# Norm rates as a ScalarE root and a VectorE reciprocal, block by block; two up tiles side by side; the last two down pieces bank by bank

## What is computed

```python
def rmsnorm(t, w, eps):                     # also rms_norm
    return t * rsqrt(mean(t * t) + eps) * w
# first block
oa  = rmsnorm(diff_attention(qa, ka, va), subln_w)          # 8 heads of 128
qkv = silu(conv5(h @ w_in[qkv columns]))                    # 24 tiles of 128 channels
q, k = l2norm(q), l2norm(k)                                 # per head, 128 wide
... gated delta rule, mixer out, x += ..., x += mixture of experts ...
# second block
yn  = (y - mu) * rsqrt(var + eps); out = (yn + bonus) * g   # RWKV mixer
x   = x + rms_norm(merged @ w_out, post_mix_g)
hf  = rms_norm(x, pre_ffn_g)
u   = square(relu(hf @ w_up)) @ w_down
out = x + rms_norm(u, post_ffn_g)
```

## Time and profile before

| what | us |
|---|---|
| runs | 2788.33, 2776.55, 2788.61 |
| median | 2788.33 |
| profiled execution, its own time | 2778.82 |
| its span | 2777.0 |
| mean granted clock of TensorE | 0.973 |

### The profile page before, as it was taken

How to read it: one execution, slowest core, us unless ns; L and a number is a source line. 1 busy time by engine, 2 the same in 40 slices (tenths; PEclk the granted TensorE clock), 3 DMA queues, 4 the chain that set the end, 5 groups by cost and what they waited for, 6 DMA issues and landing times.

```text
span 2777.0 us, 34353 instructions
## 1 busy us (share of the span) xinstructions
PE 2557.9 (92%) x14425; PEld 1728.0 (62%) x14425; DVE 1034.7 (37%) x1699; ACT 799.8 (29%) x1308; POOL 678.5 (24%) x200
## 2 busy tenths in 40 slices
PE   8999989889999999898988889989998999999998
PEld 6856777687888543333323233337676878788887
DVE  4567866765232311011011110123468563260432
ACT  6567544524222010000100000032453232411212
POOL 3400644625543000000000000023132123344442
PEclk9999989989999999999999999999998999999999
DMA  5231112103236799999999999983120023332332
GB/s 167 91 54 70 53 62 91 61 4 120 91 107 242 291 406 428 427 427 428 429 427 427 429 428 427 426 322 121 62 72 5 17 84 121 107 99 91 98 99 76
DMA packets 131342, 554.53 MB, mean 200 GB/s; under 512 B 7240, under 2 KB 88592, under 8 KB 104720
## 3 DMA queue, kind: packets, MB, share of 16 engines
q1 hardware_dynamic: 131216, 552.72, 51.3%
HBM read 542.18 MB, written 10.52 MB: 199 GB/s over the span
## 4 chain that ended last, share of the span: by engine, by line
PE 69%; DMA 13%; DVE 8%; ACT 5%; issue 3%; POOL 2%; SPq 0%; DVEq 0%; ACTq 0%
DMA S<-in_w_up 11%; PE PS L2241 8%; PE PS L612 7%; PE PS L614 7%; PE PS L613 7%; PE PS L2208 7%; PE PS L2191 2%; PE PS L3586 2%; PE PS L3589 2%; PE PS L3588 2%; PE PS L2252 1%; PE PS L2708 1%; POOL r_block L487 1%; PE PS L621 1%; DMA S<-in_w_down 1%
## 5 line engine op out<-in xcount | busy, mean ns | idle before, releaser
L2208 PE MATMUL PS<-S 128*64 128x512 f32 x2032 | 453.3, 596 | 69.9 <-DMA S<-in_w_up 66.7
L612 PE MATMUL PS<-r_block,r_block 128*128 128x512 f32 x1024 | 405.9, 396 | 13.9 <-POOL r_block L487 5.1
L2583 POOL TENSOR_TENSOR r_block<-S,r_block 128x2048 fp32r<-128x2048 f32 (+1 forms) x63 | 277.9, 4412 | 511.0 <-ACT r_block L2573 465.7
L613 PE MATMUL PS<-r_block,r_block 128*128 128x512 f32 x1024 | 400.7, 391 | 0.0
L614 PE MATMUL PS<-r_block,r_block 128*128 128x512 f32 x992 | 388.5, 392 | 0.0
L2208 PEld LDWEIGHTS PS<-S 128*64 128x64 f32 x2032 | 140.0, 137 | 374.8 <-issue 247.1
L487 POOL TENSOR_TENSOR r_block<-S,r_block 128x2048 fp32r<-128x2048 f32 x48 | 222.5, 4636 | 448.8 <-ACT r_block L479 239.6
L2437 POOL TENSOR_TENSOR S<-S 128x1024 f32<-128x1024 f32 x4 | 9.5, 2387 | 978.2 <-DVE S L2425 978.2
L2241 PE MATMUL PS<-S 128*64 128x512 f32 x1024 | 229.0, 605 | 6.0 <-DMA S<-in_w_down 2.7
L612 PEld LDWEIGHTS PS<-r_block,r_block 128*128 128x128 f32 x1024 | 193.5, 189 | 59.8 <-issue 7.6
L613 PEld LDWEIGHTS PS<-r_block,r_block 128*128 128x128 f32 x1024 | 193.6, 189 | 40.0 <-issue 0.7
(11 more groups left out here) (521 smaller groups left out, 4045.0 us busy)
## 6 DMA issues: line engine op xcount, KB each, us to landing
S<-in_w_up SPq DMA_DIRECT2D x64, 2048.0 KB, 20.8
S<-in_w_down SPq DMA_DIRECT2D x64, 2048.0 KB, 25.7
S<-in_w_gate SPq DMA_DIRECT2D x63, 2048.0 KB, 18.0
S<-in_w_in SPq DMA_DIRECT2D x57, 1024.0 KB, 5.4
S<-in_w_up SPq DMA_DIRECT2D x16, 1024.0 KB, 5.4
S<-in_w_down SPq DMA_DIRECT2D x16, 1024.0 KB, 4.9
S<-decay_rows SPq DMA_DIRECT2D x8, 1024.0 KB, 7.0
S<-in_w_out SPq DMA_DIRECT2D x8, 1024.0 KB, 5.2
```

The costliest lines, as they stand in the source:

```text
L612: pe.matmul(out, wh, r32(HT[:, dc, :]), start=(dc == 0), stop=False)
L613: pe.matmul(out, wh, r32(low[:, dc, :]), start=False, stop=False)
L2208: mm = pe.matmul(PS[c * CAP:(c + 1) * CAP, 2 + 2 * m + g, :], XE[:, 2 * q + r, e * CAP:(e + 1) * CAP], w[:, r, 1024 * g + 512 * c:1024 * g ...
L2583: pool.tensor_tensor(r32(w), w, rounded(high2(name)), ALU.subtract).then_inc(sem("w2_low"), 1)
```

## The change

At five places the rate `1 / sqrt(v + eps)` was Ln and then Exp on ACT; now it is Sqrt on ACT and a reciprocal on DVE.

- End of attention: the reciprocal stands in front of the scaling on DVE.
- Groups: at `j` 11 the root stands ahead of the middle tap on ACT, a one-element Tanh behind it. On DVE the reciprocal, the scaling of the keys and `silu(10)` stand ahead of the four taps of tile 11. The first four copies of turned tiles stand ahead of `tanh(11)`.
- Second mixer: as at the end of attention.
- Post mix norm: per row block square, root, reciprocal and addition; the product with the weights goes to another buffer (`UW`), 3 fillers instead of 12, POOL waits for the last row block before it splits ("u", 0). Up tiles 0 and 1 run together: first all products with the high part of the weights (32), then the 16 with the low part. The pre-FFN norm has root and reciprocal of 128x4.
- End: the last two down pieces go bank by bank, both over banks 0 to 4 in turn, then both for each of 5, 6 and 7. Each row block has its own rate; the last block's final step and its store are in two halves (5 stores).

```diff
@@ attention_act, attention_dve
-            act.activation(warm, eps, ACT.Ln).then_inc(sem("an_ln"), 1)
+            act.activation(warm, eps, ACT.Sqrt).then_inc(sem("an_ln"), 1)
...
-            act.activation(oln, oss, ACT.Ln, bias=eps, scale=1.0 / P).then_inc(sem("an_ln"), 1)
-            act.wait_ge(*count("an_ln", 2))
-            act.activation(ors, oln, ACT.Exp, scale=-0.5).then_inc(sem("an_r"), 1)
+            act.activation(oln, oss, ACT.Sqrt, bias=eps, scale=1.0 / P).then_inc(sem("an_ln"), 1)
...
+            dve.wait_ge(*count("an_ln", 2))
+            dve.reciprocal(ors, oln).then_inc(sem("an_r"), 1)
@@ group_act
+                if j == 11:
+                    act.activation(warm, eps, ACT.Sqrt).then_inc(sem("gn_ln"), 1)
+                    act.wait_ge(*count("gn_ss", 8 * (gr + 1)))
+                    act.activation(rnorm_l, rnorm, ACT.Sqrt, bias=eps).then_inc(sem("gn_ln"), 1)
                 act.wait_ge(*count("gp_pad", gi + 1))
...
                 if j == 11:
-                    act.wait_ge(*count("gn_ss", 8 * (gr + 1)))
-                    act.activation(rnorm_l, rnorm, ACT.Ln, bias=eps).then_inc(sem("gn_ln"), 1)
-                    act.wait_ge(*count("gn_ln", gr + 1))
-                    act.activation(rnorm, rnorm_l, ACT.Exp, scale=-0.5).then_inc(sem("gn_r"), 1)
+                    act.wait_ge(*count("gn_ln", 3 * gr + 1))
+                    act.activation(warm, eps, ACT.Tanh).then_inc(sem("gn_ln"), 1)
...
-            tanh(12 * gr + 11)
             for i in range(HG):
                 turn_back(i)
+            tanh(12 * gr + 11)
@@ group_dve
+            def scale_keys():
+                dve.wait_ge(*count("gn_ln", 3 * gr + 2))
+                dve.reciprocal(rnorm, rnorm_l).then_inc(sem("gn_r"), 1)
+                dve.wait_ge(*count("gn_r", gr + 1))
...
+                if j == 11:
+                    scale_keys()
+                    silu(10)
                 dve.wait_ge(*count("gp_copied", gi + 1))
@@ split2_pool
+            if name == ("u", 0):
+                pool.wait_ge(*count("pn1_x", TC))
@@ o2_dve
-                dve.wait_ge(*count("pn1_sq", tc + 1))
-                dve.tensor_tensor(UT[:, tc, :], UT[:, tc, :], ROWM, ALU.mult).then_inc(sem("pn1_u"), 1)
-            post_norm_dve(dve, "pn1", UT)
+                dve.wait_ge(*count("o2_copied", 4 + tc + 1))
+                dve.tensor_tensor(UW[:, tc, :], UT[:, tc, :], ROWM, ALU.mult).then_inc(sem("pn1_u"), 1)
+                post_rate_dve(dve, "pn1", tc, tc + 2)
+                dve.wait_ge(*count("pn1_u", tc + 1))
+                dve.scalar_tensor_tensor(X[:, tc, :], UW[:, tc, :], rs[:, tc:tc + 1], X[:, tc, :], ALU.mult, ALU.add)\
+                    .then_inc(sem("pn1_x"), 1)
@@ ffn_pe
-            keep_busy(pe, 0, 12)
+            keep_busy(pe, 0, 3)
...
+            def first_up_tiles():
+                wh, wl = parts2(("u", 0))
+                pe.wait_ge(*count("w2_high", turn2[("u", 0)] + 1))
+                for n in range(DC + 1):
+                    if n < DC:
+                        pe.wait_ge(*count("n4_lo", n + 1))
+                    for t, dc in ((0, n), (1, n - 1)):
+                        if 0 <= dc < DC:
+                            w = r32(wh[:, dc, P * t:P * t + P])
+                            pe.matmul(PS[:, t, :], w, r32(HT[:, dc, :]), start=(dc == 0), stop=False)
+                            pe.matmul(PS[:, t, :], w, r32(LOW4[:, dc, :]), start=False, stop=False)
+                await_split2(pe, ("u", 0))
...
+            pe.wait_ge(*count("up_lo", FT))
+            for n in range(5):
+                last_down(0, n)
+            for n in range(5):
+                last_down(1, n)
+            for n in range(5, 8):
+                last_down(0, n)
+                last_down(1, n)
@@ ffn_act, ffn_dve
             for tc in range(TC):
                 act.wait_ge(*count("dn_copied", 2 * tc + 2))
                 post_square_act(act, "pn2", UD, tc)
...
+                post_root_act(act, "pn2", tc)
...
-                if n in (1, 3, 5):
+                if n % 2:
                     weighted(n // 2)
+                if 4 <= n < 7:
+                    post_rate_dve(dve, "pn2", n - 4, n - 3)
+                    dve.wait_ge(*count("pn2_u", n - 3))
+                    finished(n - 4)
...
+            finished(3, slice(0, 512))
+            finished(3, slice(512, D))
```

113 lines of the change are left out of this document (50 added, 63 removed), and 25 rows, old and new, of the table CHAINS.

## The result

| | median, us | lowest to highest | runs |
|---|---|---|---|
| before | 2782.86 | 2776.10 to 2788.61 | 10 |
| changed | 2764.26 | 2757.27 to 2770.61 | 10 |

The ratio is 0.9929, with a 95% interval of 0.9918 to 0.9941: 19.8 us less on 2782.86, between 16.4 and 22.8 (the two medians by themselves lie 18.6 apart). The forecast was a difference of 19.4 and a time of 2768.9. The difference was right. The forecast time is 4.6 above the measured one, and that comes from the base: 2788.33 was the median of three runs, and ten runs of the kernel before have 2782.86.

A forecast was written before the change was run, and what follows sets the result against it. PE was taken as the bound, busy 2557.9 of 2777.0 us, with the weights' stream setting the pace in the experts. 0.4 + 6.0 + 0 + 9.0 + 4.0 = 19.4 us off 2788.33 gave 2768.9, range 2755 to 2778.

The forecast's parts named there:

- End of attention: Turned heads' copies on ACT start earlier without a table load and Exp: 0.4 us gained, between 0 and 1.3.
- Reciprocal of 128x32: On DVE at the end of attention and in the groups: costs 0.2 us, at most 2.5.
- Groups: End of both groups: early root lets key scaling start 3.0 us sooner each, 6.0 in all; bounds 0.7 to 3.4 each.
- Post mix norm: From post mix norm to first up tiles: row-block finishing starts the up matmuls earlier, 9.0 us gained, bounds 7.3 to 9.4.
- What hides POOL's split: First up tiles: high-part products first hide POOL's later split of the weights; without that order PE would wait 3 us.
- End: After the last bank: earlier row-block finishing and a halved last store gain 4.0 us, between 3.0 and 4.4.
- B: Mixture of experts: the weights' stream takes back the 6.4 us gained before it, leaving 13.0; chance 0.08.
- C: First up piece: POOL's split holds DVE's low parts, 3.4 us less gain, 16.0 in all; chance 0.05.
- D: Groups: two close table loads cost 1.4 us more before each root, leaving 16.6 in all; chance 0.03.
- F: Attention and groups: the 128x32 reciprocal costs 2.5 us, leaving a gain of 13.4; chance 0.03.
- G: Feed-forward after fewer fillers: the clock stays at half, making the kernel slower, 2808.9 us after 80 us of it; chance 0.05.
- E: Up tiles and one group: the clock newly falls to half for 3.4 us stretches, leaving a gain of 16.0; chance 0.06.

The follow-up runs named there:

- block 1: The changes at the end of attention and in the two groups, put alone on the kernel before; ratio 0.9981, 5.3 us less.
- the second part alone: The changes from the second mixer to the first up tiles, put alone on the kernel before; ratio 0.9968, 8.9 us less.
- the end alone: The changes to the last two down pieces, final row-block steps and stores, put alone on the kernel before; ratio 0.9989, 3.1 us less.

## Why the prediction was right, step by step

- **End of attention, 0.4.** From the root to PE's next tile it is 8.13 us, before, from the Ln, 8.34: 0.2. The split L480 starts 0.22 behind the root instead of 1.76 behind the Ln, 1.5 earlier, and 1.4 was worked out. But ACT then waits for PE's turned head:

```profile
261.08 1.27 ACT L859 ACTIVATE S<-PS,S 128x512 f32<-128x512 f32 x2 [1.21 <-PE PS L761]
```

  PE turns it no earlier, 2.64 behind root or Ln in both, as its own tiles end then. The bound named in the working, PE's turned head, is what decides, at half the size. The Tanh table's load at the first tanh of group 0 was called hidden, and it is: the pad of tile 11 keeps the 0.2.
- **Reciprocal of 128x32.** Taken as 0.2 between bounds of 0.2 and 2.5. It is 0.35, and 0.16 for 128x1 and 128x2, so 6 ns a column above a fixed part. The step that was off is the 1.1 ns a column, taken from a product: a reciprocal has nearly six times that. On 32 columns it makes 0.15, about the 0.14 by which the turned tile gains 2.86 and not 3.0.
- **Groups, 3.0 each.** 2.86 at PE's first turned tile in both. At the first chunk product it depends on where the half clock falls behind PE's wait: 9.09 to 10.69 behind the pad in the seven traces with all of block 1's change as it stands, before and in the four other kernels without it 12.28 to 13.78, medians 2.8 apart; in the second group 3.0 by the medians. The working had the last silu at 339.6 and just in time; it was 339.07 to 339.76, with PE at L1463 from 340.12. Timed alone, block 1 has 5.3 us with an interval from 2.5 to 8.4, and the difference of the ratios with and without it is 6.4.
- **Second mixer, 0.** The stretch from L3385 to the last copy is 152.69 us before and 152.74 in the changed kernel.
- **Post mix norm, 9.0.** 9.36, and 9.52 to the end of the span. Two of its steps were off: the 32 transposes take 3.67 us, not 4.4, and L563 is released by ACT's own split and not by PE, so that it starts 4.04 behind the copy instead of 4.6. That is 0.56 more gain than the 8.8 worked out for the first up matmul, and the forecast came near by the 0.2 that it added for the clock. And the added wait of POOL, on which a paragraph was spent, never acts: POOL's idle ends with ACT's split (`<-ACT r_block L2582`), which ends after X is complete.
- **What hides POOL's split.** "Without it PE would wait 3 us" was right for the wait (3.86 idle, 3.0 late), and left out the clock, another 2.7.
- **End, 4.0.** 3.74 in the whole, 3.53 alone. Both have 3.97 behind the start of the last addition. In the whole 0.23 go off for a last bank that comes later than with the second part alone, the 0.2 of the working. With the end alone 0.44 go off, and these aren't the end's: its first up matmul stands 15.48 behind the copy, and from there to the last bank it is as in the kernel before (352.87 and 352.89).
- **The base.** Three runs, two near 2788 and one at 2776.6, were read as two levels. Ten runs fill the space between. A forecast of the difference was safe; the absolute one should have said that its base was uncertain by 6 us.
- **Rivals.** B, C, D, F and G did not come: the experts' length is the same and they begin 6.3 us earlier in the mean, L574 takes 0.67 beside POOL, the table loads again end 0.02 ahead of the next instruction (330.06 + 1.28, next at 331.36), the reciprocal is 0.35, and the clock stays up with no filler at all. E came in a weaker form: nothing fell at the up tiles, but in the groups and in the mixers both kernels have stretches at half the clock whose length varies from execution to execution.

## To carry to other kernels

A value that is needed late but known early is worth moving as far forward as its inputs allow, and with it the work that it releases: root and reciprocal alone brought nothing in the groups, the new place all. Before a wait is filled with dummy work, look whether the operands can come in pieces; then look whether part of the operands (here the high parts) is enough to start, since here an idle of 3.9 us cost 3.0 by its length and another 2.7 by the clock. And when two traces differ by less than the sum of their places, compare the places from a near event, and the rest with a third and fourth execution before explaining it. The trace with block 1 alone would have confirmed the wrong rival; the kernels with the same text in that place showed that its loss was the execution's.
